# Attention of an encoder layer: scores with keys on partitions in place of turned softmax rows, and row maxima taken from the high halves

## The reference

```python
h = _rmsnorm(x, norm1) @ w_in
c_q, c_kv, k_rope, u = h[..., :o1], h[..., o1:o2], h[..., o2:o3], h[..., o3:]
q = jnp.einsum('bsr,rhd->bshd', _rmsnorm(c_q, q_a_norm), w_q_b)
kv = jnp.einsum('bsr,rhd->bshd', _rmsnorm(c_kv, kv_a_norm), w_kv_b)
...
s = jnp.einsum('bqhd,bkhd->bhqk', qn, k_nope) + jnp.einsum('bqhd,bkd->bhqk', qr, k_rope)
pr = jax.nn.softmax(s.astype(jnp.float32) * scale, axis=-1).astype(v.dtype)
return jnp.einsum('bhqk,bkhd->bqhd', pr, v)
...
x = x + jnp.concatenate([attn, pool], axis=-1) @ w_out
```

## Time and profile before

| | |
|---|---|
| median of 3 runs | 1142.33 us |
| profiled execution | 1145.8 us, span 1144.0 us |
| PE busy in the span | 98%, at a granted clock of 0.994 |
| DVE, ACT, POOL busy | 73%, 49%, 41% |
| chain that ended last, PE's share | 84% |

### The profile page before, as it was taken

The page is one execution under the profiler, slowest core; times in us unless marked ns, Lnnn a source line. Parts: engine busy times, 40 slices in busy tenths (PEclk is TensorE's granted clock), DMA queues, the critical chain, the costliest instruction groups (busy, mean ns, idle before and its releaser), DMA issues.

```text
span 1144.0 us, 15838 instructions
## 1 busy us (share of the span) xinstructions
PE 1117.0 (98%) x5146; PEld 898.0 (78%) x5146; DVE 833.3 (73%) x1171; ACT 555.3 (49%) x986; POOL 466.8 (41%) x405
## 2 busy tenths in 40 slices
PE   8999999999999989999999999999999999999996
PEld 7788766665878867888888888888888888888885
DVE  6895976674468799878787878787876756757555
ACT  5412687775223454545454445444554545544332
POOL 0186642322567046765686568655220202211000
PEclk9999999999999999999999999999999999999999
DMA  6601000104653126443544354444896565534341
GB/s 208 222 26 44 1 12 12 38 19 168 200 185 120 56 64 220 165 139 136 194 165 138 138 193 165 138 141 173 326 349 205 186 200 189 180 100 127 92 143 74
DMA packets 138431, 161.60 MB, mean 141 GB/s; under 512 B 8755, under 2 KB 105354, under 8 KB 133770
## 3 DMA queue, kind: packets, MB, share of 16 engines
q1 hardware_dynamic: 138080, 160.82, 42.1%
q10 hardware_dynamic: 298, 0.11, 0.0%
HBM read 115.55 MB, written 45.35 MB: 141 GB/s over the span
## 4 chain that ended last, share of the span: by engine, by line
PE 84%; DVE 11%; issue 2%; ACT 1%; POOL 1%; DMA 1%; ACTq 0%; DVEq 0%; POOLq 0%
PE ps L312 26%; PE ps L313 25%; PE ps L314 25%; PE ps L885 2%; PE ps L866 2%; DVE WL L2076 1%; DVE SF L2175 1%; DVE SF L2183 1%; PE ps L877 1%; DVE XL L1745 1%; DVE WDHL L1933 1%; DMA TL<-g_scratch 1%; DVE col L1944 1%; DVE XT L1739 0%; DVE R L1926 0%
## 5 line engine op out<-in xcount | busy, mean ns | idle before, releaser
L312 PE MATMUL ps<-XH,WH 128*128 128x512 f32 x722 | 284.0, 393 | 1.4 <-DVE WL L353 1.0
L314 PE MATMUL ps<-XH,WL 128*128 128x512 f32 x722 | 281.4, 390 | 0.0
L313 PE MATMUL ps<-XL,WH 128*128 128x512 f32 x722 | 281.3, 390 | 0.0
L312 PEld LDWEIGHTS ps<-XH,WH 128*128 128x128 f32 x722 | 135.9, 188 | 31.1 <-DVE WL L353 1.8
L314 PEld LDWEIGHTS ps<-XH,WL 128*128 128x128 f32 x722 | 135.6, 188 | 28.5
L313 PEld LDWEIGHTS ps<-XL,WH 128*128 128x128 f32 x722 | 135.9, 188 | 27.2
L312 PE MATMUL ps<-GHL,WH 128*128 128x512 f32 x394 | 153.7, 390 | 1.0 <-DVE WL L2076 0.7
L314 PE MATMUL ps<-GHL,WL 128*128 128x512 f32 x394 | 153.3, 389 | 0.0
L313 PE MATMUL ps<-GHL,WH 128*128 128x512 f32 x394 | 153.3, 389 | 0.0
L348 ACT ACTIVATE WH<-WR 128x1024 fp32r<-128x1024 f32 (+3 forms) x45 | 45.5, 1012 | 135.8 <-PE ps L314 122.7
L1492 ACT ACTIVATE SF<-ps,col 128x512 f32<-128x512 f32 x88 | 68.2, 778 | 74.7 <-PE ps L314 65.6
(11 more groups left out here) (259 smaller groups left out, 2263.7 us busy)
## 6 DMA issues: line engine op xcount, KB each, us to landing
TL<-in_w_up SPq DMA_DIRECT2D x48, 256.0 KB, 3.5
s_scratch<-XT SPq DMA_DIRECT2D x11, 1024.0 KB, 4.7
XT<-in_w_down SPq DMA_DIRECT2D x11, 1024.0 KB, 6.5
t_scratch<-XT SPq DMA_DIRECT2D x11, 1024.0 KB, 3.8
WR<-t_scratch SPq DMA_DIRECT2D x44, 256.0 KB, 2.8
TL<-s_scratch SPq DMA_DIRECT2D x44, 256.0 KB, 2.9
WR<-in_w_up SPq DMA_DIRECT2D x40, 256.0 KB, 3.4
WR<-in_w_down SPq DMA_DIRECT2D x33, 256.0 KB, 3.5
```

What stands on the lines that cost most here:

```text
L312: pe.matmul(out, wh, xh, start=first, stop=False, skip_group_check=skip)
L313: pe.matmul(out, wh, xl, start=False, stop=False, skip_group_check=skip)
L314: return pe.matmul(out, wl, xh, start=False, stop=last, skip_group_check=skip)
```

## The change

The scores are made with the operands exchanged, so that keys lie on partitions and queries along a row. The exponentiated block then is already what `weigh` needs, and ACT writes it straight into `XT`; the transposes (L866) and ACT's copies (L1326) go. A row maximum would now lie across partitions. So:

- PE makes each block a second time in the old orientation from the high halves alone (`rough`, one matmul), and DVE reduces it (`maximum`), three units ahead.
- For each head and sequence (16 in all) PE turns the four columns of maxima in one matmul with 4 output rows (`turn_max`), ACT writes them in four small copies of 4x128 into four more rows of `QH` (`max_rows`), each scaled with a column of `ident` so that one row holds one block's maxima. `KH` has ones in those four rows, set by POOL at the start of the program. The first matmul of `scores` takes 100 rows in place of 96 and so subtracts the maxima. `scores(v - 2)` is issued in the unit in which `rough(v + 3)` is.
- The row sums are no longer ACT's: POOL adds the four blocks of each head (`key_sum`, three 128x512 additions), two matmuls with ones sum over partitions (`total`), DVE turns the 32x32 blocks of the result, inverts one column of each, ACT spreads it (`spread_rc`), DVE turns it back and multiplies (`scale_rows`). POOL's diagonals go.
- From the second pair on POOL makes the low halves of the queries (`q_low`), which DVE did; `latent_low` of the second sequence moves there too.
- POOL's last pooling (`windows`) for both sequences comes ahead of its `keep_low`s. DVE makes the maxima of units 4n+2 and 4n+3 both in unit 4n. The first projections (`project_k`, `project_q`) are issued 6 matmuls ahead of the end of the input product, and six products of the first output tile are moved into the last pair (units 7, 8, 10, 12, 14, 15).

```diff
         PT = XT[:, :].rearrange("p (a k q) -> p a k q", a=4, k=TT)
-        PB = [SF[:, 0:512], SF[:, 512:1024], SF[:, 4608:5120]]
+        SUM = [SF[:, 2560:3072], diag[:, :, :].rearrange("p t q -> p (t q)"), SF[:, 0:512], SF[:, 512:1024]]
+        RT = SF[:, 4608:5120]
         VB = [v.rearrange("p (k d) -> p k d", d=P) for v in (SF[:, 3072:4096], SF[:, 1536:2560])]
         QF = R
         QTMP = SQT
-        DR = [SF[:, 2560:3072], diag[:, :, :].rearrange("p t q -> p (t q)")]
...
+                            pe.wait_ge(c_lo, 2)
+                            pe.wait_ge(kr_done, 4)
+                            project_k(0, 0, mix_hi, 6)
+                            pe.wait_ge(c_lo, 4)
+                            project_q(0, 0, acc_free, 14)
                             in_tile(a, s, range(6, KT))
...
-            def scores(i, u):
-                j, t = divmod(u, TT)
-                s, h = divmod(j, 2)
+            def rough(v):
+                n, t = divmod(v, TT)
+                s, h = divmod(n % 4, 2)
                 if t == 0:
-                    pe.wait_ge(q_lo, i * 4 + j + 1)
-                    pe.wait_ge(k_lo, i * 4 + j + 1)
-                if i * 16 + u >= 3:
-                    pe.wait_ge(exp_done, i * 16 + u - 2)
-                tok = slice(t * P, (t + 1) * P)
-                ins = mm3(pe, s_bank(i * 16 + u)[:, :], QH[0:HEAD, s, h, tok], QL[0:HEAD, s, h, tok],
-                          KH[0:HEAD, s, h, :], KL[0:HEAD, s, h, :], True, True)
-                ins.then_inc(s_ready, 1)
-            def turn(i, u):
-                pe.wait_ge(exp_done, i * 16 + u + 1)
-                if i == 0 and u < 2:
-                    pe.wait_ge(v_copied, u + 1)
+                    pe.wait_ge(q_hi, n + 1)
+                    pe.wait_ge(k_hi, n + 1)
+                if v >= 2:
+                    pe.wait_ge(max_ready, v - 1)
+                pe.matmul(m_bank(v)[:, :], QH[0:HEAD, s, h, t * P:(t + 1) * P], KH[0:HEAD, s, h, :],
+                          start=True, stop=True).then_inc(m_ready, 1)
+            def turn_max(n):
+                pe.wait_ge(max_ready, 4 * n + 4)
+                if n:
+                    pe.wait_ge(max_row, n)
                 else:
-                    pe.wait_ge(pt_ready, i * 16 + u - 1)
-                for k in range(TT):
-                    ins = pe.transpose(ps[4 + u % 2][:, k * P:(k + 1) * P], p_buf(i * 16 + u)[:, k * P:(k + 1) * P], ident[:, :])
-                ins.then_inc(p_tr, 1)
+                    pe.wait_ge(acc_free, 14)
+                    pe.wait_ge(consts_set, 5)
+                pe.matmul(ps[1][0:TT, 0:P], MXR[:, n % 2, 0:TT], ident_r[:, :], start=True, stop=True).then_inc(max_turned, 1)
+            def scores(v):
+                n, k = divmod(v, TT)
+                s, h = divmod(n % 4, 2)
+                if k == 0:
+                    pe.wait_ge(max_row, n + 1)
+                    pe.wait_ge(q_lo, n + 1)
+                    pe.wait_ge(k_lo, n + 1)
+                if v < 2:
+                    pe.wait_ge(v_copied, v + 1)
+                else:
+                    pe.wait_ge(exp_done, v - 1)
+                keys = slice(k * P, (k + 1) * P)
+                o = s_bank(v)[:, :]
+                pe.matmul(o, KH[0:MAXED, s, h, keys], QH[0:MAXED, s, h, :], start=True, stop=False)
+                pe.matmul(o, KH[0:HEAD, s, h, keys], QL[0:HEAD, s, h, :], start=False, stop=False)
...
-                    pe.wait_ge(v_copied, i * 2 + s + 1 + (i < HEADS // 2 - 1) * 2)
-                    for h in range(2):
-                        ins = pe.matmul(ps[7][h * V_DIM:(h + 1) * V_DIM, :], ones[:, 0:V_DIM], DR[h], start=True, stop=True)
-                    ins.then_inc(rr_ready, 1)
-                    pe.wait_ge(pt_ready, i * 16 + 8 * (s + 1))
                     if i or s:
                         pe.wait_ge(o_norm, i * 2 + s)
+                    pe.wait_ge(v_copied, i * 2 + s + 1)
+                pe.wait_ge(exp_done, i * 16 + 8 * s + 4 + ks[-1] + 1)
...
+                pe.wait_ge(sum_step, 3 * (i * 4 + 2 * s + 2))
+                if i or s:
+                    pe.wait_ge(rr_copied, i * 2 + s)
+                pe.wait_ge(v_copied, i * 2 + s + 1 + (i < HEADS // 2 - 1) * (2 - s))
+                for h in range(2):
+                    ins = pe.matmul(ps[7][h * V_DIM:(h + 1) * V_DIM, :], ones[:, 0:V_DIM], SUM[2 * s + h], start=True, stop=True)
+                ins.then_inc(rr_ready, 1)
...
-                        scores(i, u + 3)
-                    elif not last:
-                        scores(i + 1, u + 3 - 4 * TT)
+                    v = 4 * TT * i + u
+                    if v == 1:
+                        turn_max(0)
+                    if v + 3 < 2 * HEADS * TT:
+                        rough(v + 3)
+                    if u % TT == 1 and v > 1:
...
+            def exponent(v):
+                n, k = divmod(v, TT)
+                act.wait_ge(s_ready, v + 1)
+                if v in (8, 12):
+                    act.wait_ge(d_lo, 7 if v == 8 else 8)
+                    act.wait_ge(keep_lo, 3 if v == 8 else 6)
+                if k == 0 and n >= 4:
+                    act.wait_ge(o_ready, n // 2 - 1)
+                    act.wait_ge(sum_step, 3 * (n - 3))
+                act.activation(PT[:, (n + 2) % 4, k, :], s_bank(v)[:, :], ACT.Exp).then_inc(exp_done, 1)
+            def max_rows(n):
+                s, h = divmod(n % 4, 2)
+                act.wait_ge(max_turned, n + 1)
+                if n >= 4:
+                    act.wait_ge(s_ready, 4 * (n - 3))
+                for a in range(TT):
+                    ins = act.activation(QH[HEAD:MAXED, s, h, a * P:(a + 1) * P], ps[1][0:TT, 0:P], ACT.Copy,
+                                         scale=ident[0:TT, a:a + 1])
+                ins.then_inc(max_row, 1)
+            def spread_rc(i, s):
+                act.wait_ge(rc_ready, 2 * (i * 2 + s) + 1)
+                act.activation(RT.rearrange("p (b c) -> p b c", c=32), col[:, RC:RC + 16].unsqueeze(2).broadcast_to([P, 16, 32]),
+                               ACT.Copy).then_inc(o_hi, 1)
...
-            def maximum(i, u):
-                dve.wait_ge(s_ready, i * 16 + u + 1)
-                dve.tensor_reduce(col[:, NB + u % 4:NB + u % 4 + 1], s_bank(i * 16 + u)[:, :], AX_X, ALU.max,
-                                  negate=True).then_inc(max_ready, 1)
+            def maximum(v):
+                n, k = divmod(v, TT)
+                dve.wait_ge(m_ready, v + 1)
+                dve.tensor_reduce(MXR[:, n % 2, k:k + 1], m_bank(v)[:, :], AX_X, ALU.max, negate=True).then_inc(max_ready, 1)
             def inverse(i, s):
-                dve.wait_ge(exp_done, i * 16 + 8 * (s + 1))
-                if i:
-                    dve.wait_ge(dr_ready, i * 2 + s - 1)
-                dve.reciprocal(col[:, RC + 8 * s:RC + 8 * s + 8], col[:, RS + 8 * s:RS + 8 * s + 8]).then_inc(rc_ready, 1)
+                n = i * 2 + s
+                dve.wait_ge(rr_ready, n + 1)
+                dve.transpose(RT, ps[7][:, :]).then_inc(rr_copied, 1)
+                dve.wait_ge(rr_copied, n + 1)
+                dve.reciprocal(col[:, RC:RC + 16].unsqueeze(2), RT.rearrange("p (b c) -> p b c", c=32)[:, :, 0:1]).then_inc(rc_ready, 1)
             def scale_rows(i, s):
-                dve.wait_ge(o_ready, i * 2 + s + 1)
-                dve.wait_ge(rr_copied, i * 2 + s + 1)
+                n = i * 2 + s
+                dve.wait_ge(o_hi, 2 * n + 1)
+                dve.transpose(RB[:, :], RT).then_inc(rc_ready, 1)
+                dve.wait_ge(o_ready, n + 1)
+                dve.wait_ge(rc_ready, 2 * n + 2)
                 dve.tensor_tensor(RB[:, :], ps[6][:, :], RB[:, :], ALU.mult).then_inc(o_norm, 1)
...
-                        maximum(i, u + 2)
-                    elif not last:
-                        maximum(i + 1, u + 2 - 4 * TT)
+                    v = 4 * TT * i + u
+                    if v == 0:
+                        rotate(0, 1)
+                        maximum(1)
...
+            for c in range(2):
+                pool.wait_ge(c_hi, 4 + c + 1)
+                pool.tensor_tensor(CHL[:, 1, c, 1, :], cs[:, c, 1, :], CHL[:, 0, c, 1, :].bitcast(F32), ALU.subtract).then_inc(c_lo, 1)
...
+            def q_low(n, summed):
+                s, h = divmod(n % 4, 2)
+                pool.wait_ge(q_hi, n + 1)
+                pool.wait_ge(q_lo, n)
+                pool.wait_ge(sum_step, summed)
+                pool.tensor_tensor(QL[0:HEAD, s, h, :], QF[0:HEAD, n % 2, :], QH[0:HEAD, s, h, :].bitcast(F32), ALU.subtract).then_inc(q_lo, 1)
+                pool.wait_ge(q_lo, n + 1)
+            def key_sum(n, k):
+                a, buf = PT[:, (n + 2) % 4], SUM[n % 4]
+                pool.wait_ge(exp_done, 4 * n + k + 1)
+                if k == 1:
+                    if n >= 4:
+                        pool.wait_ge(rr_ready, n // 2 - 1)
+                    pool.tensor_tensor(buf, a[:, 0, :], a[:, 1, :], ALU.add).then_inc(sum_step, 1)
+                else:
```

(14 more changed lines are left out.)

484 lines of the change are left out of this document (246 added, 238 removed).

## The result

The changed kernel takes **1150.28 us** (median of 4 runs, 1149.30 to 1150.54) against 1142.28 for the kernel before (4 runs, 1141.71 to 1144.97): ratio 1.0056 [1.0041, 1.0071], slower. Beside the experiments, in five rounds, the same kernel gave 1149.71 against 1143.86: 1.0048 [1.0034, 1.0061].

What follows compares the result with a forecast made beforehand. PE's own issue was taken to bound steady pairs, DVE the first pair. First pair +1.6, steady pairs -1.1 and last pair +2.0 sum to 2.5 us more: 1148.3 profiled, 1144.8 for the median; range 1136.5 to 1151.

Steps and rivals of the forecast that it cites:

- no difference: Whole kernel: time within 3.4 us (0.3%) of no change, forecast 1144.8 us; chance 0.38.
- Entry and first pair: From the input product's end through the first pair: DVE holds up the second turn, 169.4 against 167.77, 1.6 us more.
- Steady pair: Each steady head pair: issue plus new waits of 2.05 make 37.4 us against 37.95; 1.1 us less for two.
- My terms for the wait at unit 1: Start of a pair: DVE's fourth maximum ready at 4.95 us, PE arrives at 4.1, so a wait of 0.85.
- 35.35 us of issue: PE in a steady pair: summed matmul groups 35.2 plus 0.15 carried for what the sum misses, waits not included.
- Last pair and exit: Last pair up to the output product: issue 38.1, waits 4.1, less 2.1; 40.1 against 38.14, 2.0 us more.
- Prices: Assumed instruction times: PE's turn of maxima 0.12 us, DVE's turn 0.65, row copies 0.20 each, POOL's additions 1.27.
- The estimate of 1.24 us: DVE's 128x512 turn, as four times the skill's 311 ns for 128x128 in 16 bits; sum some 2 us higher.
- The chains hide: Rival, attention pairs: ACT and DVE run ahead and the waits go; 8.8 us less, 1133.5 us; chance 0.27.
- The longer turn of the maxima: Rival, PE's first scores of each head: longer row copies and DVE turn, 1152.7 us, a half 1149; chance 0.22.
- POOL as the bound: Rival, POOL in the pairs: additions at 2.0 us give 1150, at 2.15 some 1157; decides from 1.9; chance 0.13.
- The rule that I set beside it: POOL shares SBUF interfaces with DVE, contending with two-SBUF-input or two-port DVE instructions; maxima harmless, few weight splits not.

Runs made afterwards that it cites:

- run 8: Changed kernel plus short filler matmuls on PE at its waits in the first pair, up to unit 9: 1147.47 us, ratio 1.0027.
- run 9: Changed kernel with POOL's keep_low(0) and keep_low(2) ahead of the last windows again, as before the change: 1146.84 us, ratio 1.0026.
- run 11: Changed kernel with scale_rows behind the maxima, query projections earlier, POOL's low halves first, values(1, 0) behind the first weigh, short fillers: 1143.55 us, ratio 0.9991.
- runs 3: Changed kernel with DVE's scale_rows at unit 0 moved behind the maximum that turn_max waits for: 1148.23 us, ratio 1.0038.
- run 5: Changed kernel with scale_rows at units 0 and 8 behind the maximum, query projections moved from units 7 and 14 to 5 and 13: 1142.51 us, ratio 0.9986.

## Why the prediction was right or wrong

The range held the time by 0.7 us; the likeliest case, "no difference", did not. I forecast 2.5 us more profile against profile, and the section shows 4.3. The mechanism was right, new waits that eat the shorter issue; a term of its sum was mis-sized. By my own steps, from the start of a pair's unit 0 (169.66 us for the second pair, so 245.7 for the last):

- **Entry and first pair, +1.6: measured +1.45** (51.3 us from the section's start against 49.9). Right in size, wrong in make-up. I had one wait of 5 us for DVE before the second turn. DVE was the bound, as said (9.75 of 10 us in 130:140), but PE's waits ahead of that turn came in pieces (1.0, 0.2, 1.35, 0.5), and it came 19.9 us behind the section's start where I had 22.6, so 2.7 earlier. The rest of the pair took 31.4 us where I had 28.9, so that the two errors nearly cancel, by luck. In that rest lie waits for a split of weights (1.2) and for `values` (1.6), and what I had not priced: the half clock, up to 1.5 us (run 8), and POOL's new order, 1.2 (run 9), an edit that I had not costed at all. Whether the two add up no run shows: run 11 undoes both, but it carries the moves too, and its clock fell at another place.
- **Steady pair, 37.4: measured 38.03.** The waits were right, 0.81, 0.64, 0.64 and none at unit 9, 2.1 against my 2.05; runs 3 and 5 show that they are on the path in full. (My terms for the wait at unit 1 add up to 4.85, not the 4.95 that I wrote, and so give 0.75.) The step that failed is the **35.35 us of issue**: run 5 shows 35.95. In its rows a `weigh` is 1.87, not 1.81, and a `total` 1.01, not 0.91, 0.4 us for a pair. I took the distance to the next turn's start as the length of 32-bit groups, and the rest of the sum by rounded figures. That is 0.6 in each pair, and turned 1.1 us less into 0.15 more for two.
- **Last pair and exit, +2.0: measured +2.7.** Waits 4.07 against my 4.1, but otherwise spread: 0.3 us more at units 8 and 9, and 0.15 of the 0.4 before the last `weigh`. The missing 0.7 is then issue again, by subtraction; no run measured it by itself.
- **Prices**: turn of maxima 0.06 plus 0.05 behind it (taken 0.12); DVE's turn 0.71 (0.65 taken, 1.18 the bound). The estimate of 1.24 us from the Trainium skill (VectorE: DVE Perf Modes, The three transpose paths) did not hold for these 32-bit turns of 128x512. Row copies 1.1 for four against 0.8; POOL's additions 1.28 to 1.33 against 1.27.
- **Rivals.** *The chains hide* fell: the waits are there. *The longer turn of the maxima* had the right sign and a time near the measured one (1149), by the wrong cause: the turn was as priced, and the extra came from issue. *POOL as the bound* fell: additions at 1.3, 26.4 us a pair, and in run 5 a pair of 35.95 with POOL at 26.9. The rule that I set beside it (the Trainium skill, GPSIMD Engine Reference, Specifications) agrees with the trace from the other side: POOL's additions hardly suffered in a steady pair, but a DVE instruction with two SBUF inputs did in the first one, 1.76 us instead of 0.68.

So where did the gain go? A steady pair has 35.95 us of issue on PE instead of 37.94, 2.0 less, and new waits of 2.1: all of it went into waiting for the turned maxima. The 4.3 us are lost at both ends, 1.45 in the first pair and 2.7 in the last.
